# Filter taps joined in the array's rows, Hyena projections moved among the long convolutions, and attention maxima taken negated

## The chip, the core and the metric

One core of a Trainium2 chip (8 cores). The metric is the device time of one execution of the whole program in microseconds, the median of several runs. TensorE is PE in the profile, VectorE DVE, ScalarE ACT, GpSimd POOL, and SP is the queue that loads weights.

## The reference

Two transformer blocks run one after the other on 512 tokens of width 1024, all in float32. The parts that matter here lie in the second block.

Differential attention (4 heads, two maps each) over 256 context and 512 own keys:

```python
s = einsum("bhmqd,bhmkd->bhmqk", q, k) * (64 ** -0.5)     # 0.125
a = softmax(s)
w = a[:, :, 0] - lam * a[:, :, 1]
o = einsum("bhqk,bhkd->bhqd", w, v)                        # then rmsnorm, a gain
```

The Hyena mixer: a projection to 1536 columns (12 groups of 128, named 0 to 11 below), a short convolution of 3 taps, then a split into v, x1, x2 (groups 0 to 3, 4 to 7, 8 to 11) and two orders of a gated long convolution:

```python
for n, gate in enumerate((x1, x2)):
    z = gate * (long_conv(z, k_f[:, n]) + p["hy_skip"][n] * z)
```

Its filters come from a small network: 33 features of 512 positions, three layers of width 64 with a sine, and a last matrix 64 x 2048 (2 orders, 2 directions, 512 channels), times a decay. The filters do not depend on x, so they can be made at any time.

## The kernel before, in words

**Arithmetic and weights.** Big matrix products are made of fp32r matmuls. Each operand is a high part and a low part, and `mm3` issues three matmuls (high·high, high·low, low·high). Weights come in units of 128 x 1024 in one fixed order (`plan`, line 27), through four RAW buffers and four slots of WH and WL. SP loads RAW, ScalarE copies it to WH (line 1081, `wh`), and VectorE (line 1651) or GpSimd (line 2274) writes `wl` = RAW − WH. Which of the two does it is the list POOL_LOW (line 155). ScalarE, VectorE and GpSimd walk the units in order and stay SLOTS − 1 = 3 units ahead of TensorE. The DFT matrices of the long convolutions come already split (kind "pre", list PRE) and are loaded straight to WH and WL by GpSimd's queue (`load_pre`, line 2280), which waits until TensorE has begun the unit three before. Each engine has its program written out in its own order; semaphores join them.

**PSUM banks.** `bank(key, s, n, among)` (line 434) takes the next bank of a ring in fixed rotation and waits until semaphore `s` says that the bank's last user is drained. In the long convolutions there are two rings, RING4 = banks 0 to 3 and ACC = banks 4 to 7; Hyena groups 0 to 9 use RING2 = (6, 7).

**Filters (first block, 25 to 115 us).** While TensorE makes the projections of the first block, one step `first(k)` (24 fp32r matmuls) is followed by one step `second(k)`: three `filter_layer` (line 557, fp32, 64 output rows, 64 columns of weights), then eight `taps(i, o)` (line 567). Each of these has two fp32 matmuls of K = 64, 128 output rows and 512 columns, both from partitions 0 to 63. An fp32 matmul stands as two passes in the trace. VectorE multiplies by the decay (line 1718), GpSimd adds and subtracts the two directions (line 2311), SP stores them.

**Differential attention (945 to 1052 us).** 16 cycles n, one for each head and block of 128 queries. TensorE: `diff_scores(n)` (line 882; 64-row pairs, m = 0 and 1, into banks 0+1 and 2+3, free again after the exponentials), `diff_turn(n − 2)` (six transposes), two quarters of a Hyena group (12 matmuls, `hyena_part`, line 913), and once in four cycles `diff_values`. VectorE: `diff_max(n)` (line 2057: maximum of 768 scores, times −0.125, for each of the two maps), at times the split of a weight unit or `hyena_conv` (line 2078, the short convolution of a group in place in TMP), then `diff_weights(n)` (line 2066: `em` = em0 + r·em1, two SBUF inputs). ScalarE: `exp(0.125·s + bias)` (line 1444). GpSimd is idle. Eight groups (0 to 7) are done here.

**Long convolutions (1052 to 1166 us).** `hyena_turn(j)` transposes the convolved group j, ScalarE copies it to U. `fold(o)` makes even and odd parts `ED` of z, high and low (VectorE, ScalarE, GpSimd). Then for each order o and quarter f: `forward(o, f)` (12 matmuls, two RING4 banks, drained by the first four products), `spectral` on VectorE (line 2147: four products, a difference, a sum), high part `ysh` on ScalarE, low part `ysl` on GpSimd, and `backward(o, f)` (12 matmuls into the four ACC banks) two quarters later. At the end of an order z = gate · (...) on VectorE and GpSimd, then fold again. In between stand the attention output's scaling (`sub_sums`: 32 matmuls of one column; `sub_scale(h)`: one fp32 matmul with the diagonal `ndg` from ScalarE) and the Hyena groups 8 to 11 (`hyena_group`, line 937). TensorE's order before is:

```
turns 0-3, group 8, turns 4-7, sub_sums, group 9, turn 8
order 0: fw0 sc0 fw1 fw2 bw0 fw3 turn9 sc1 bw1 group10 bw2 bw3 group11 sc2
order 1: fw0 turn10 sc3 fw1 fw2 bw0 fw3 turn11 bw1 bw2 bw3
output projection: first half (48 matmuls), transposes of xn, second half
```

Of the kernel before, what the change touches and what calls it, by code (L numbers as in the profile page):

```python
# [9 lines left out]
P = 128  # L10
S = 512
D = 1024
# [6 lines left out]
BEFORE = 10  # L19
# [8 lines left out]
def plan():  # L28
# [69 lines left out]
    for o in range(2):  # L98
# [4 lines left out]
        if o == 0:  # L103
            pack(colmajor("w_in_2", 1536 + 10 * P, 1))
        pack(inv[2] + inv[3], "pre")
        if o == 0:
            pack(colmajor("w_in_2", 1536 + 11 * P, 1))
# [39 lines left out]
for _u in range(NU):  # L147
# [9 lines left out]
    AT["dft_f", 0, 0][0][0] + SLOTS - 1 <= u < AT["w_out_2", 0, 0][0][0] + SLOTS - 1  # L157
# [8 lines left out]
class Waits:  # L166
# [5 lines left out]
    def wait_ge(self, name, n):  # L172
        s, before = self.find(name)
        if n > 0 and self.past.get(s.name, 0) < before + n:
# [35 lines left out]
          "v_score": (("sb_sp", 32), ("df_mx", 64)),  # L210
# [61 lines left out]
def program(nc, a):  # L272
    ctx = ExitStack()
    with ctx:
# [54 lines left out]
        W4 = at("w4", 168, [64, CHUNK])  # L329
# [95 lines left out]
        def tensor_program(engine):  # L425
# [131 lines left out]
            def filter_layer(l):  # L557
# [405 lines left out]
            for j in range(4):  # L963
                hyena_turn(j)
            hyena_group(8)
            for j in range(4, 8):
                hyena_turn(j)
            sub_sums()
            hyena_group(9)
            hyena_turn(8)  # L970
# [24 lines left out]
            for o in range(2):  # L995
                for f in range(4):
                    forward(o, f)
                    if f == 0:
                        if o:
                            hyena_turn(10)  # L1000
                        sub_scale(3 * o)
                    if f == 3:
                        hyena_turn(9 + 2 * o)
                        if o == 0:
                            sub_scale(1)
                    if f >= 2:
                        backward(o, f - 2)
                if o == 0:
# [58 lines left out]
        def scalar_program(engine):  # L1067
# [65 lines left out]
            def second(k):  # L1133
                if k < 3:
                    e.wait_ge("f_red", 7 * k + 7)
                    act(TMP[0:64, (4, 5, 4)[k], :], TMP[0:64, 3, :], ACT.Sin).then_inc(sem("f_sin"), 1)
# [246 lines left out]
            def rotated(r):  # L1383
                e.wait_ge("rp_add", 2 * r + 2)
                dh = QTh[:, r, :] if r < 4 else KTh[:, r - 4, 256:]
                act(dh, T(2 + r % 3), ACT.Copy).then_inc(sem("qk2_hi"), 1)
# [51 lines left out]
            def diff_scores(n):  # L1438
                for m in range(2):
                    b = BANK["ds", 2 * n + m]  # L1440
                    s = PS[:, b:b + 2, :].rearrange("p a n -> p (a n)")[:, 0:768]
                    e.wait_ge("df_mx", 4 * n + 2 * m + 2)
                    e.wait_ge("p_dt", n - 1)
                    act(EM[n % 2][m][:, :], s, ACT.Exp, scale=0.125, bias=ND[n % 4][:, m:m + 1],  # L1444
# [52 lines left out]
            weights(unit("w_in_2", 0, 1536 + 8 * P) + SLOTS - 1)  # L1497
            conv_center(8)
# [4 lines left out]
            weights(unit("w_in_2", 0, 1536 + 9 * P) + SLOTS - 1)  # L1503
            conv_center(9)
            hyena_turn(8)
# [9 lines left out]
            for o in range(2):  # L1515
                for f in range(4):
                    weights(unit("dft_f", 128, f * P, o) + SLOTS - 1)
                    spectral(4 * o + f)
                    if f == 0:
                        if o:  # L1520
                            hyena_turn(10)
# [3 lines left out]
                    if f == 3:  # L1525
                        hyena_turn(9 + 2 * o)
                        if o == 0:
                            sub_high(1)
                            sub_diag(2)
                    if f >= 2:  # L1530
                        weights(unit("dft_i", 0, 0, o) + SLOTS - 1 if f == 2 else unit("dft_i", P, 0, o) + SLOTS - 1)
                if o == 0:
                    weights(unit("w_in_2", 0, 1536 + 10 * P) + SLOTS - 1)
                weights(unit("dft_i", 3 * P, 0, o) + SLOTS - 1)
                for i in range(2):
# [1211 lines left out]
```

## Time and profile before

| | |
|---|---|
| median of 3 runs | 1582.85 us (1582.1 to 1583.59) |
| profiled execution | 1580.21 us |
| its span, first to last instruction | 1578.5 us |
| mean granted TensorE clock | 0.991 of full speed |
| TensorE matmuls | 1507.5 us busy (96%), 6878 |
| VectorE | 877.3 us (56%), 1429 |
| ScalarE | 622.5 us (39%), 978 |
| GpSimd | 291.1 us (18%), 289 |
| memory | 187.87 MB moved, mean 119 GB/s |

Busy time is the time in which at least one instruction of the engine was running. TensorE's matmuls overlap, so the length of one is more than the distance between two; what one costs is the distance between starts. A number in square brackets behind a row is the idle time ahead of it and what ended it. `TMP<-PS,pp,TMP x6` is one short convolution, `TMP<-PS,kf x4` the four products of a spectral step.

### The profile page before, as it was taken

The numbers are of one execution on the slowest core, as the hardware profiler recorded it, in microseconds if no ns is written. First come the engines' busy times: TensorE is split into PE (matmuls) and PEld (weight loads), VectorE is DVE, ScalarE is ACT, GpSimd is POOL, SyncE is SP. The second block draws the span as 40 slices with busy tenths as digits, with TensorE's granted clock in tenths as the row PEclk, the third lists the DMA queues.
The fourth block names the chain that finished last, engine by engine and source line by source line (L and its number), as shares of the span: only waits on it lengthen the run. The fifth ranks groups of instructions, "written<-read, shape, count | busy, mean of one in ns | idle before, by whom it ended". The sixth has DMA issues, their size and how long they took to land.

```text
span 1578.5 us, 17718 instructions
## 1 busy us (share of the span) xinstructions
PE 1507.5 (96%) x6878; PEld 1200.0 (76%) x6878; DVE 877.3 (56%) x1429; ACT 622.5 (39%) x978; POOL 291.1 (18%) x289
## 2 busy tenths in 40 slices
PE   6999999999989999999997998989798999999998
PEld 5767667888868878888886876668576888888886
DVE  5445556555467654565447438856766455334534
ACT  5535664222353322334335325644344333223332
POOL 0253111110122200122004310006441110111101
PEclk9999999999999999999999999999999999999999
DMA  7342002654345544545326221124442322323221
GB/s 232 126 146 81 27 28 93 235 166 148 132 134 173 174 147 140 178 145 178 113 100 208 91 67 40 41 94 139 131 154 69 108 93 95 99 89 106 94 94 54
DMA packets 53262, 187.87 MB, mean 119 GB/s; under 512 B 6104, under 2 KB 6616, under 8 KB 52986
## 3 DMA queue, kind: packets, MB, share of 16 engines
q1 hardware_dynamic: 47386, 165.76, 32.3%
q0 software_dynamic: 4736, 16.78, 3.2%
q10 hardware_dynamic: 1056, 4.19, 0.7%
q8 instruction: 55, 0.90, 0.2%
q14 instruction: 29, 0.24, 0.0%
HBM read 174.12 MB, written 12.58 MB: 118 GB/s over the span
## 4 chain that ended last, share of the span: by engine, by line
PE 80%; DVE 9%; issue 4%; ACT 4%; POOL 3%; DMA 0%; SPq 0%; DVEq 0%; POOLq 0%; ACTq 0%
PE PS L447 79%; POOL TMP L2311 2%; DVE smallring L2062 1%; DVE TMP L2083 1%; PE PS L458 1%; ACT em L1444 1%; DVE wl L1651 1%; DVE TMP L2158 1%; DVE em L2076 1%; POOL y L2321 0%; DMA X<-in_x 0%; ACT wh L1081 0%; DVE accm L1631 0%; ACT wt L1435 0%; POOL wl L2274 0%
## 5 line engine op out<-in xcount | busy, mean ns | idle before, releaser
L1651 DVE TENSOR_TENSOR wl<-raw,wh 128x1024 fp32r<-128x1024 f32 x219 | 283.8, 1299 | 283.1 <-ACT wh L1081 283.0
L447 PE MATMUL PS<-HTh,wh 128*128 128x512 f32 x1056 | 419.7, 397 | 12.4 <-DVE TMP L1977 5.8
L447 PE MATMUL PS<-HTh,wl 128*128 128x512 f32 x1056 | 413.0, 391 | 0.0
L447 PE MATMUL PS<-HTl,wh 128*128 128x512 f32 x1056 | 412.8, 391 | 0.0
L1081 ACT ACTIVATE wh<-raw 128x1024 fp32r<-128x1024 f32 x228 | 239.1, 1053 | 286.2 <-PE PS L447 251.9
L447 PEld LDWEIGHTS PS<-HTh,wh 128*128 128x128 f32 x1056 | 199.5, 189 | 61.3 <-issue 11.0
L447 PEld LDWEIGHTS PS<-HTh,wl 128*128 128x128 f32 x1056 | 199.0, 188 | 42.8
L447 PEld LDWEIGHTS PS<-HTl,wh 128*128 128x128 f32 x1056 | 199.5, 189 | 38.5 <-issue 0.5
L447 PE MATMUL PS<-wh,FFh 128*128 128x512 f32 x432 | 169.1, 392 | 0.0
L447 PE MATMUL PS<-wh,FFl 128*128 128x512 f32 x432 | 168.2, 389 | 0.0
L447 PE MATMUL PS<-wl,FFh 128*128 128x512 f32 x432 | 168.1, 389 | 0.0
L1631 DVE SCALAR_TENSOR_TENSOR accm<-raw,small,accm 128x256 f32<-128x256 f32 x224 | 108.0, 516 | 3.4
L2234 DVE SCALAR_TENSOR_TENSOR TMP<-PS,pp,TMP 128x255 f32<-128x255 f32 (+1 forms) x132 | 52.1, 395 | 80.3 <-ACT TMP L1583 76.4
L447 PEld LDWEIGHTS PS<-wh,FFl 128*128 128x128 f32 x432 | 81.1, 188 | 17.1
L447 PEld LDWEIGHTS PS<-wl,FFh 128*128 128x128 f32 x432 | 81.1, 188 | 16.5
L447 PEld LDWEIGHTS PS<-wh,FFh 128*128 128x128 f32 x432 | 81.1, 188 | 16.5
L2384 POOL TENSOR_TENSOR FFl<-TMP,FFh 128x512 fp32r<-128x512 f32 x32 | 41.6, 1299 | 240.1 <-ACT FFh L1295 240.1
L2466 POOL TENSOR_TENSOR FFl<-TMP,FFh 128x512 fp32r<-128x512 f32 x22 | 28.5, 1294 | 211.8 <-ACT FFh L1590 211.8
L1295 ACT ACTIVATE FFh<-TMP 128x512 fp32r<-128x512 f32 x32 | 20.2, 632 | 66.5 <-DVE TMP L1917 66.5
L1291 ACT ACTIVATE TMP<-PS 128x512 f32<-128x512 f32 x32 | 19.0, 595 | 57.7 <-PE PS L447 57.7
L2083 DVE SCALAR_TENSOR_TENSOR TMP<-PS,pp,TMP 128x255 f32<-128x255 f32 (+1 forms) x72 | 28.4, 395 | 16.0 <-ACT TMP L1452 13.9
L2474 POOL TENSOR_TENSOR X<-X,TMP 128x512 f32<-128x512 f32 x14 | 19.7, 1434 | 90.1 <-DVE TMP L2249 90.1
(320 smaller groups left out, 2163.7 us busy)
## 6 DMA issues: line engine op xcount, KB each, us to landing
raw<-in_ws SPq DMA_DIRECT2D x268, 512.0 KB, 3.8
taps<-TMP SPq DMA_DIRECT2D x16, 256.0 KB, 2.5
tab<-in_spec POOLq DMA_DIRECT2D x8, 512.0 KB, 5.6
raw<-taps SPq DMA_DIRECT2D x8, 512.0 KB, 3.7
kd<-TMP POOLq DMA_DIRECT2D x16, 256.0 KB, 4.3
wh<-in_wd POOLq DMA_DIRECT2D x8, 512.0 KB, 3.9
wl<-in_wd POOLq DMA_DIRECT2D x8, 512.0 KB, 4.6
kf<-kd SPq DMA_DIRECT2D x8, 512.0 KB, 3.9
```

The lines of the kernel that those rows point to most:

```text
L447: return nc.tensor.matmul(out, l, r, start=start, stop=stop, skip_group_check=True)
L1081: act(WH[u % SLOTS][:, :n], RAW[i % RAWS][:, :n], ACT.Copy).then_inc(sem("w_hi"), 1)
L1291: act(T(q % 2), PS[:, BANK["ff", hf, m], :], ACT.Relu).then_inc(sem("ff_relu"), 1)
L1295: act(FFh[:, m, :], T(2 + q % 2), ACT.Copy).then_inc(sem("ff_hi"), 1)
L1631: stt(acc, r[:, k % 4, :], c, acc, ALU.mult, ALU.add).then_inc(sem("mod_acc"), 1)
L1651: tt(WL[k][:, :n], RAW[RAW_AT["unit", u, 0] % RAWS][:, :n], f32(WH[k][:, :n]), ALU.subtract).then_inc(sem("lo_dve"), 1)
L2083: stt(out[:, do], ps[:, di], pp("hy_conv_w_2", 12 * w + j), out[:, do], ALU.mult, ALU.add).then_inc(sem("hc_v"), 1)
L2234: stt(z[:, do], ps[:, di], pp("ffn_conv_w_2", 22 * w + m), z[:, do], ALU.mult, ALU.add).then_inc(sem("uc_v"), 1)
L2311: tt(T(k), T(3), T(5), op).then_inc(sem("tap_ed"), 1)
L2384: tt(FFl[:, q % 16, :], T(2 + q % 2), f32(FFh[:, q % 16, :]), ALU.subtract).then_inc(sem("ff_lo"), 1)
L2466: tt(FFl[:, m - first_m, :], T(m % 4), f32(FFh[:, m - first_m, :]), ALU.subtract).then_inc(sem("ug_lo"), 1)
L2474: tt(x, x, T(4 + q % 4), ALU.add).then_inc(sem("dn_xp"), 1)
```

## The change

1. **Taps.** The three layers' weights are laid twice side by side, so that each layer gives 128 output rows, the lower 64 a copy of the upper. The last matrix is laid out as 128 x 1024: direction 0 in partitions 0 to 63, direction 1 in 64 to 127. `taps(i, o)` takes both banks first and then issues one matmul from each half of the partitions.
2. **Maxima.** `reduce_max(..., negate=True)` writes the negated maximum, and the multiply by −0.125 is gone (32 instructions). The queries carry the 0.125 (a scale in an existing copy and in an existing subtraction).
3. **Hyena groups 8 to 11.** Group 8 goes to order 0 ahead of bw2; 9 and 10 behind bw3; 11 to order 1 ahead of bw2. The turns, the short convolutions and the units of weights follow. TensorE's new order:

```
turns 0-7, sub_sums
order 0: fw0 sc0 fw1 fw2 bw0 fw3 sc1 bw1 group8 bw2 bw3 turn8 group9 group10 sc2
order 1: fw0 sc3 fw1 turn9 fw2 turn10 bw0 fw3 bw1 group11 bw2 bw3 turn11
```

   On VectorE convolution 8 stands behind spectral step 3, 9 behind fold(1) and sub_high(2), 10 behind spectral step 4 and sub_high(3), 11 behind spectral step 7.
4. **POOL_LOW** begins at the first Hyena unit + 3 instead of the first DFT unit + 3.

```diff
 POOL_LOW = [u for u in range(NU) if u not in PRE and (
-    AT["dft_f", 0, 0][0][0] + SLOTS - 1 <= u < AT["w_out_2", 0, 0][0][0] + SLOTS - 1
+    AT["w_in_2", 0, 1536][0][0] + SLOTS - 1 <= u < AT["w_out_2", 0, 0][0][0] + SLOTS - 1
...
-        W4 = at("w4", 168, [64, CHUNK])
+        W4 = at("w4", 168, [P, D])
...
-                mm(PS[0:64, b, :], TMP[0:n, 1, 64 * l:64 * l + 64], src, True, True).then_inc(sem("p_filt"), 1)
+                mm(PS[:, b, :], TMP[0:n, 1, P * l:P * (l + 1)], src, True, True).then_inc(sem("p_filt"), 1)

             def taps(i, o):
+                n = 4 * i + 2 * o
                 for d in range(2):
-                    n = 4 * i + 2 * o + d
-                    b = bank(("tap", n), "tap_mul", n + 1, RING2)
-                    c = o * 1024 + d * 512
-                    e.wait_ge("f_sin", 3)
-                    e.wait_ge("d_w4", 48)
-                    mm(PS[:, b, :], TMP[0:64, 4, i * P:(i + 1) * P], W4[:, c:c + 512], True, True).then_inc(sem("p_tap"), 1)
+                    bank(("tap", n + d), "tap_mul", n + d + 1, RING2)
+                e.wait_ge("f_sin", 3)
+                e.wait_ge("d_w4", 48)
+                for d in range(2):
+                    pr = slice(64 * d, 64 * d + 64)
+                    mm(PS[:, BANK["tap", n + d], :], TMP[pr, 4, i * P:(i + 1) * P], W4[pr, o * S:(o + 1) * S], True,
+                       True).then_inc(sem("p_tap"), 1)
...
             def hyena_group(j):
-                bank(("hy", j), "hc_v", 6 * j + 6, RING2 if j < 10 else RING4)
+                bank(("hy", j), "hc_v", 6 * j + 6, ACC if j == 10 else RING4)
...
                     if f == 0:
-                        if o:
-                            hyena_turn(10)
                         sub_scale(3 * o)
-                    if f == 3:
-                        hyena_turn(9 + 2 * o)
-                        if o == 0:
-                            sub_scale(1)
+                    if f == 3 and o == 0:
+                        sub_scale(1)
+                    if f in (1, 2) and o:
+                        hyena_turn(8 + f)
                     if f >= 2:
                         backward(o, f - 2)
-                if o == 0:
-                    hyena_group(10)
+
+                hyena_group(8 + 3 * o)
                 backward(o, 2)
                 backward(o, 3)
+                hyena_turn(8 + 3 * o)
                 if o == 0:
-                    hyena_group(11)
+                    hyena_group(9)
+                    hyena_group(10)
                     sub_scale(2)
...
-                    nc.vector.reduce_max(r[:, m:m + 1], s, axis=mybir.AxisListType.X).then_inc(sem("df_mx"), 1)
-                    e.wait_ge("df_mx", 4 * n + 2 * m + 1)
-                    ts(r[:, m:m + 1], r[:, m:m + 1], -0.125, None, ALU.mult).then_inc(sem("df_mx"), 1)
+                    nc.vector.reduce_max(r[:, m:m + 1], s, axis=mybir.AxisListType.X, negate=True).then_inc(sem("df_mx"), 1)
...
                     spectral(4 * o + f)
                     if f == 0:
                         sub_high(3 * o)
+                    if f == 0 and o:
+                        hyena_conv(10)
                     if f == 3 and o == 0:
                         sub_high(1)
+                hyena_conv(8 + 3 * o)
                 e.wait_ge("p_bw", 4 * o + 4)
```

## Rows read from the trace of the kernel before

**Rows 1.** The page, part 1: busy us (share of the span) and instructions.

```profile
PE 1507.5 (96%) x6878; PEld 1200.0 (76%) x6878; DVE 877.3 (56%) x1429; ACT 622.5 (39%) x978; POOL 291.1 (18%) x289
```

**Rows 2.** Waits of TensorE: us in total, times, longest us.

```profile
PE PS L447 <- ACT em L1444: 7.8, 9, 1.0
...
PE PS L447 <- DVE TMP L2083: 6.0, 2, 5.0
...
PE PS L447 <- POOL ysl L2432: 3.0, 1, 3.0
```

**Rows 3.** Chain that ended last: start us, us, what.

```profile
760.38 8.20 PE PS L447 x36
```

**Rows 4.** Windows: PE, PEld, DVE, ACT, POOL busy, PEclk, DMA share, GB/s.

```profile
80.00:120.00 40.00, 40.00 (x151) 27.28 (x150) 18.11 (x22) 13.62 (x15) 22.24 (x17) 1.00 0.45 145
```

**Rows 5.** Timeline of PE around a pair of taps: start us, us, instruction.

```profile
65.16 1.98 PE L447 MATMUL PS<-w,TMP 64*128 64x512 f32 x4
67.07 0.50 PE L447 MATMUL PS<-HTh,wh 128*128 128x512 f32 x1
```

**Rows 6.** Timeline of PE around the pool's mixing.

```profile
131.77 1.07 PE L447 MATMUL PS<-pt,wpool 64*64 64x512 f32 x4
132.77 0.50 PE L447 MATMUL PS<-wh,HTh 128*128 128x512 f32 x1
```

**Rows 7.** Timeline of PE in attention, scores of two cycles.

```profile
998.10 0.50 PE L447 MATMUL PS<-KTh,QTh 64*128 64x512 f32 x2
...
1003.97 0.50 PE L447 MATMUL PS<-KTh,QTh 64*128 64x512 f32 x2 [1.01 <-ACT em L1444]
```

**Rows 8.** Timelines of DVE and ACT in the same cycle.

```profile
999.67 1.02 DVE L2076 SCALAR_TENSOR_TENSOR em<-em,smallring,em 128x768 f32<-128x768 f32 x1
1000.60 0.95 DVE L2062 TENSOR_REDUCE smallring<-PS 128x1 f32<-128x768 f32 x1
...
1001.66 0.95 DVE L2062 TENSOR_REDUCE smallring<-PS 128x1 f32<-128x768 f32 x1
...
997.84 1.06 ACT L1081 ACTIVATE wh<-raw 128x1024 fp32r<-128x1024 f32 x1
...
1002.83 0.90 ACT L1444 ACTIVATE em<-PS,smallring 128x768 f32<-128x768 f32 x1
```

**Rows 9.** Line 2274, GpSimd's splits: duration ns min/median/max.

```profile
L2274 POOL TENSOR_TENSOR wl<-raw,wh x9: 2358/2387/2844, 445.7 to 1151.7; 128x1024 fp32r<-128x1024 f32 x9
```

**Rows 10.** Line 1631, and timelines of DVE and POOL at 515 us.

```profile
L1631 DVE SCALAR_TENSOR_TENSOR accm<-raw,small,accm x224: 470/478/1526, 266.7 to 770.0; 128x256 f32<-128x256 f32 x112
...
515.01 2.55 DVE L1631 SCALAR_TENSOR_TENSOR accm<-raw,small,accm 128x256 f32<-128x256 f32 x3
...
515.45 1.30 POOL L2384 TENSOR_TENSOR FFl<-TMP,FFh 128x512 fp32r<-128x512 f32 x1 [3.88 <-ACT FFh L1295]
```

**Rows 11.** Timeline of PE, turns 0 to 3 and the transposes of xn.

```profile
1057.21 1.91 PE L458 MATMUL PS<-cst,TMP 128*128 128x128 f32 x16
...
1164.31 1.91 PE L458 MATMUL PS<-cst,xn 128*128 128x128 f32 x16
```

**Rows 12.** Timeline of PE in between, two waits and a slow matmul.

```profile
1071.12 0.63 PE L447 MATMUL PS<-HTl,wh 128*128 128x512 f32 x1
...
1126.95 2.07 PE L447 MATMUL PS<-ndg,cst 128*128 128x512 f32 x2 [5.01 <-DVE TMP L2083]
...
1150.58 0.50 PE L447 MATMUL PS<-ysh,wh 128*128 128x512 f32 x1 [3.05 <-POOL ysl L2432]
```

**Rows 13.** Timeline of DVE, a short convolution and four products.

```profile
1124.35 2.54 DVE L2083 SCALAR_TENSOR_TENSOR TMP<-PS,pp,TMP 128x255 f32<-128x255 f32 x6 [2.53 <-ACT TMP L1452]
1126.81 2.47 DVE L2158 TENSOR_TENSOR TMP<-PS,kf 128x512 f32<-128x512 f32 x4
```

**Rows 14.** Timelines of ACT and PE around the start of order 1.

```profile
1107.06 1.09 ACT L1537 ACTIVATE TMP<-PS 128x512 f32<-128x512 f32 x2 [5.14 <-PE PS L447]
...
1119.39 0.50 PE L447 MATMUL PS<-EDh,wh 128*128 128x512 f32 x1 [0.41 <-POOL EDl L2417]
```

More of the change, by code:

```diff
@@ L18 @@
 AHEAD = 8
-BEFORE = 10
+BEFORE = 8
 MAGIC = 12582912.0
@@ L961, in sub_scale @@
                 mm(PS[:, b, :], ONES, NDG[:, :], True, True).then_inc(sem("p_sn"), 1)
[L963 to L966, printed above, removed]
+            for j in range(8):
                 hyena_turn(j)
             sub_sums()
-            hyena_group(9)
-            hyena_turn(8)
             def forward(o, f):
@@ L1524, in scalar_program @@
                             sub_diag(1)
[L1525 to L1529, printed above, removed]
+                    if f == 3 and o == 0:
+                        sub_high(1)
+                        sub_diag(2)
+                    if f in (1, 2) and o:
+                        hyena_turn(8 + f)
                     if f >= 2:
                         weights(unit("dft_i", 0, 0, o) + SLOTS - 1 if f == 2 else unit("dft_i", P, 0, o) + SLOTS - 1)
-                if o == 0:
-                    weights(unit("w_in_2", 0, 1536 + 10 * P) + SLOTS - 1)
+                weights(unit("w_in_2", 0, 1536 + (8 + 3 * o) * P) + SLOTS - 1)
+                conv_center(8 + 3 * o)
                 weights(unit("dft_i", 3 * P, 0, o) + SLOTS - 1)
+                hyena_turn(8 + 3 * o)
                 for i in range(2):
@@ L1539, in scalar_program @@
                     fold(1)
-                    conv_center(10)
-                    weights(unit("w_in_2", 0, 1536 + 11 * P) + SLOTS - 1)
+                    weights(unit("w_in_2", 0, 1536 + 9 * P) + SLOTS - 1)
+                    conv_center(9)
+                    weights(unit("w_in_2", 0, 1536 + 10 * P) + SLOTS - 1)
                     sub_high(2)
                     sub_diag(3)
-                    conv_center(11)
+                    conv_center(10)
             e.wait_ge("p_bw", 8)
@@ L2014, in rotated @@
                 e.wait_ge("qk2_hi", r + 1)
-                tt(dl, T(2 + r % 3), f32(dh), ALU.subtract).then_inc(sem("qk2_lo"), 1)
+                if r < 4:
+                    stt(dl, T(2 + r % 3), 0.125, f32(dh), ALU.mult, ALU.subtract).then_inc(sem("qk2_lo"), 1)
+                else:
+                    tt(dl, T(2 + r % 3), f32(dh), ALU.subtract).then_inc(sem("qk2_lo"), 1)
             for m in range(4):
@@ L2125, in vector_program @@
             fold(0)
-            weights(unit("w_in_2", 0, 1536 + 8 * P) + SLOTS - 1)
-            hyena_conv(8)
             ps, fits, r, q = PS[:, BANK["sub"], 0:16], SUBR[:, 0:16], SUBR[:, 16:32], SUBR[:, 32:48]
@@ L2143, in vector_program @@
             stt(q, q, 1024.0, R0, ALU.mult, ALU.mult).then_inc(sem("sub_v"), 1)
-            weights(unit("w_in_2", 0, 1536 + 9 * P) + SLOTS - 1)
-            hyena_conv(9)
             def spectral(n):
@@ L2439, in gpsimd_program @@
                         weights(unit("dft_i", 0, 0, o) + SLOTS - 1 if f == 2 else unit("dft_i", P, 0, o) + SLOTS - 1)
-                if o == 0:
-                    weights(unit("w_in_2", 0, 1536 + 10 * P) + SLOTS - 1)
                 weights(unit("dft_i", 3 * P, 0, o) + SLOTS - 1)
                 e.wait_ge("ac_v", 4 * o + 2)
-                e.wait_ge("u_ev", 4 * o + 8)
+                e.wait_ge("u_ev", 8 if o == 0 else 12)
                 tt(U[:, 2, 0:512], T(4), U[:, 2, (o + 1) * S:(o + 2) * S], ALU.mult).then_inc(sem("z_p"), 1)
@@ L2447, in gpsimd_program @@
                     fold(1)
-                    weights(unit("w_in_2", 0, 1536 + 11 * P) + SLOTS - 1)
+                    weights(unit("w_in_2", 0, 1536 + 9 * P) + SLOTS - 1)
+                    weights(unit("w_in_2", 0, 1536 + 10 * P) + SLOTS - 1)
                     sub_low(2)
@@ L2584, in sync_program @@
             load_spectrum(1)
-            weights(unit("w_in_2", 0, 1536 + 9 * P) + SLOTS - 1)
             for n in range(8):
@@ L2593, in sync_program @@
                 if n == 3:
-                    weights(unit("w_in_2", 0, 1536 + 11 * P) + SLOTS - 1)
+                    weights(unit("w_in_2", 0, 1536 + 10 * P) + SLOTS - 1)
             weights(unit("w_out_2", 7 * P, S) + SLOTS - 1)
@@ L2731 @@
         "lam": np.concatenate([i[n].reshape(-1) for n in ("lam_q1_2", "lam_q2_2", "lam_k1_2", "lam_k2_2")]),
-        "hy_w1_2": i["hy_w1_2"][0], "hy_w2_2": i["hy_w2_2"][0], "hy_w3_2": i["hy_w3_2"][0],
-        "hy_w4_2": i["hy_w4_2"][0],
-    }
+        "hy_w4_2": i["hy_w4_2"][0].reshape(64, 2, 2, S).transpose(2, 0, 1, 3).reshape(P, D),
+    }
+    for n in ("hy_w1_2", "hy_w2_2", "hy_w3_2"):
+        arrays[n] = np.tile(i[n][0], (1, 2))
     arrays = {k: np.ascontiguousarray(v) for k, v in arrays.items()}
```

38 lines of the change are left out of this document (13 added, 25 removed).

## The prediction

> **What bounds the kernel now.** I started with the page: TensorE (PE) is busy 1507.5 of 1578.5 us, VectorE (DVE) 877 [rows 1]. So a microsecond taken off TensorE's own work, where it never waits, is a microsecond of the end, and the rest of what can be won is in its few waits. Then the waits by releaser, of which the change bears on three: 7.8 us for ScalarE's exponentials `em`, 6.0 us for VectorE's short convolutions (L2083), 3.0 us for GpSimd's `ysl` [rows 2]. A full fp32r matmul of 512 columns costs TensorE 0.228 us (36 in 8.20 us), however long its own bar is [rows 3]. Last, the timelines of three places: the filters' taps (65 to 111 us), differential attention (945 to 1052), the long convolutions (1057 to 1164).
>
> **Taps of the filters.** From 80 to 120 us TensorE is busy in all 40.00 us [rows 4], so its work there is the path. Two taps are four passes over the same 64 rows: the next matmul starts 67.07 − 65.16 = 1.91 us later [rows 5]. The nearest thing to the new form is the pool's mixing, also two fp32 matmuls of 512 columns from partitions 0 to 63 and 64 to 127, in the order pass, pass, pass, pass: 132.77 − 131.77 = 1.00 us for the four [rows 6]. It has other columns too, the taps have not; but the scores of attention are 64x128 pairs of exactly the taps' form, and there the two of a pair stand as "x2" at one start in 0.50 us together, five more such pairs behind them [rows 7]. Eight pairs × 0.91 = **7.3 us** off. Bounds: 0 (no overlap) and 8.0. The second bank is now waited for before the first matmul; it was drained while the whole projection before it ran (24 × 0.228 = 5.5 us), so nothing waits behind it. VectorE's filter steps on 128 partitions instead of 64, ScalarE's sines, and three wider loads cost the same per column and are hidden: 0. GpSimd's sums of taps follow the taps and move with them.
>
> **Maxima negated as taken.** Each of 32 small multiplies holds VectorE from one `reduce_max` to the next: 1001.66 − 1000.60 = 1.06 us, of a 0.95 us instruction whose follower could start 0.09 before its end, so 0.87 without. The second exponential starts at 1002.83 and TensorE's scores at 1003.97 after a wait of 1.01 [rows 8, 7]. Without both multiplies and with ScalarE's own 0.88 between exponentials, it starts some 0.36 us earlier from the same first maximum, and 0.27 more where two cycles hang on each other. Beside this the diff widens POOL_LOW: its lower end goes from the first DFT unit + 3 to the first Hyena unit + 3. So the five splits of Hyena units 3 to 7, in the midst of attention, go from VectorE to GpSimd, and those of units 8 and 9 leave attention with their units. Followed cycle by cycle, the waits on `em` shrink by 0.6 at four places, by 0.3 to 0.4 at two: **3.2 us** off, if GpSimd does not hurt. The 0.125 on the queries is folded into an existing copy and subtraction outside any wait: 0.
>
> **What GpSimd's splits take back.** One takes it 2.39 us [rows 9]. GpSimd is idle in attention, so by itself this is hidden. But a VectorE instruction with two SBUF inputs stops while GpSimd reads: three `accm` steps took 2.55 us from 515.01, with a GpSimd subtraction from 515.45 to 516.75; such a step is 0.478 us at the median and 1.526 at most [rows 10]. The weighting `em<-em,smallring,em` (L2076) is of that kind, 0.95 us, and on the path (it stands ahead of the next maxima). In the cycles with a convolution, ScalarE's `wh` begins at 997.84 and takes 1.06, GpSimd would start at 998.98 and read until 1001.4, and `em` starts at 999.67, after the change 0.27 earlier: 999.40, some 0.4 us behind GpSimd, and waits: 2.0 us late [rows 8, 9]. The pattern repeats: I find this order at three of the five `wh` rows of the stage (units 4, 5 and 7; the row shown is unit 7's) and the reverse at two (3 and 6), where GpSimd waits and nobody is late. 3 × 1.95 = 5.85 us. Attention is then 5.85 − 3.2 = **2.65 us slower**. The bounds are −3.2 (none) and +6.5 (all five, at 1.95).
> By the Trainium skill, "SBUF — State Buffer", section "Who interferes with whom", a VectorE instruction with two SBUF inputs contends with a GpSimd instruction that reads SBUF, and whichever issues first holds the port for the whole instruction; by that rule the price is the same 2 us each, and the trace's 1.526 us rows agree.
>
> **The long convolutions.** Turns 0 to 3 start at 1057.21, the transposes `xn` at 1164.31: 107.1 us [rows 11]. The work in between is 336 matmuls (four groups of 24, eight forwards and eight backwards of 12, 48 of the output projection) × 0.228 = 76.5, twelve turns 5.0, sub_sums 3.5, four sub_scales 3.7: 88.7. So 18.4 us are lost, mainly a wait of 5.01 before sub_scale(3), 3.05 before backward(1,2), and a stretch of 0.43 us a matmul instead of 0.23 at the lower clock (1.2 instead of 2.4 GHz) after sub_sums' small matmuls [rows 11, 12]. None of the 88.7 is removed; only the order is new.
> I laid the new order out against these durations: convolution of a group 2.54, products of a spectral step 2.47 (step about 4) [rows 13], ScalarE's copy of a turn 0.5.
> Start: with groups 8 and 9 gone, turns 4 to 7 wait for ScalarE's copies (1.3), the first forward for banks and the low halves (0.5), sub_scale(0) for `ndg`, which comes some 5.5 us after sub_sums ends (four turn copies and a table load now stand ahead of it on ScalarE, and group 9 no longer covers it). The low clock falls into the same gap. Loss 4.5.
> Order 0: group 8 covers spectral step 3, groups 9 and 10 with sub_scale(2) are 11.9 us of work after backward(0,3). What forward(1,0) needs came until 1119.39 after a copy begun at 1107.06 [rows 14]; 12.3 us; turn 8's copy, now ahead of it on ScalarE, makes it 13.4. That is the last low half, which the forward needs 2.1 us after its start, at 14.0. Covered, by 0.6: 0.
> Order 1: the four-bank ring decides. In the new order sub_scale(3) takes the bank after forward(1,0), so forward(1,1) straddles: its second half takes forward(1,0)'s first bank and waits 0.9 for the products; forward(1,2) takes sub_scale's (0.3) and then forward(1,1)'s first, free only after spectral step 5's products. VectorE now does convolution 9, step 4, sub_high(3), convolution 10, and only then step 5: 13.5 us. That wait is 3.6. Loss 4.8. The output projection's banks wait for turn 11's copy: 0.7. The end's chain (copy, products, norm) has 11 us of matmuls above it, as now.
> New losses 10.0 instead of 18.4: **8.3 us** off. Unknown ones: a ring wait of 0 to 7 us, a low clock of up to 2 us more; 5 to 12. GpSimd's loads of the DFT halves stand behind fold(1) and group 10's split; they land 4.6 us after issue, just in time.
>
> **The sum.** The profiled execution took 1580.2 us around a span of 1578.5; the median of three runs is 2.6 above it. −7.3 + 2.65 − 8.3 = −12.95: 1567.3 profiled, 1569.9 against 1582.85.
>
> **The rivals.** (a) *GpSimd never catches `em`.* It is 0.35 to 0.45 us early in my layout, so a small shift undoes it. Then 1569.9 − 5.85 = 1564.1. Chance 0.27. (b) *The taps do not overlap* (no pair of fp32 passes on 64x128 stands in the trace): 1577.2. Chance 0.05. (c) *VectorE sets the pace of order 1*, with both convolutions and its two-SBUF sums held up by GpSimd as in [rows 10]. Two or three blocks of 2 us more than I laid out are 4 to 5 us: 1574.5. Chance 0.09. (d) *Slower:* TensorE's clock falls after sub_sums and, with gaps where groups 8 and 9 stood, does not come back for some time. Each matmul then costs 0.2 more; 65 of them eat the gain, 81 make it 0.2% slower. Before, eight or nine like the one shown were slow there [rows 12]. All 288 to the end of order 1 would be 1627. Chance 0.02. The forecast itself: 0.57. That the change does less than it says is (b).
>
> **How the numbers follow.** The point is the forecast's, 1569.9. The range takes in (a) with its unknowns and the forecast's own spread by the order-1 wait, 1562 to 1574; outside are (b), (d), half of (c) and the tails. A measurement of this kernel can tell about 0.2% (3.2 us) from no change. Every case but (d) and a coincidence of (b) and (c) is faster by more: 0.96, 0.02 and 0.02.
>
> **What would show it.** Right: taps rows at 1.0 us before the next matmul; five GpSimd `wl` rows in attention, three of 16 L2076 rows near 3 us; PE waits on `em` of 2 us at two or three places; no wait before sub_scale(3) for L2083, but one of some 3.6 us for L2158 in forward(1,2); turns to `xn` in about 99 us. Wrong: all L2076 rows at 1.02 us; taps still 1.9; a row of slow matmuls past 1080.

## The result, and the profile after

The changed kernel takes 1574.3 us at the median (1570.36 to 1576.92, six runs) beside 1582.86 (1582.1 to 1583.59, six runs): ratio 0.9945, 95% interval 0.9933 to 0.9958, so 8.6 us faster. I had said 12.95 us, 1569.9 us, and a range of 1562 to 1574: the sign was right, the size was not, and the median lies just above the range. The profiled execution took 1573.92 us around a span of 1572.2. Between the two profiled executions the span falls by 6.3 us only, from 1578.5 us.

The page's first part, busy time and instructions, answers to [rows 1]:

```profile
PE 1508.3 (96%) x6878; PEld 1201.7 (76%) x6878; DVE 868.3 (55%) x1390; ACT 623.6 (40%) x978; POOL 307.6 (20%) x296
```

TensorE's busy time has not fallen, though the taps alone should have taken 7 us off it. That is the first sign that matmuls elsewhere became longer. GpSimd has 16.5 us more: seven more splits at about 2.4 us, five of them in attention and two in the long convolutions, where the units of groups 8 and 9 now fall. The waits of TensorE (total, times, longest) answer to [rows 2]:

```profile
PE PS L446 <- ACT em L1442: 9.7, 8, 2.2
...
PE PS L446 <- ACT TMP L1359: 3.9, 1, 3.9
PE PS L446 <- DVE TMP L2147: 3.9, 3, 3.2
```

The waits of 5.0 us for the short convolutions and of 3.0 us for `ysl` are gone, as meant. In their place stand 3.9 us for the products of a spectral step, and the wait for `em` has grown from 7.8 to 9.7 with a longest one of 2.2 instead of 1.0.

**Taps.** TensorE's timeline around the second and the last pair, which answers to [rows 5]:

```profile
63.28 1.13 PE L446 MATMUL PS<-w,TMP 64*128 64x512 f32 x4
64.34 0.50 PE L446 MATMUL PS<-HTh,wh 128*128 128x512 f32 x1
...
103.72 1.13 PE L446 MATMUL PS<-w,TMP 64*128 64x512 f32 x4
104.78 0.50 PE L446 MATMUL PS<-HTh,wh 128*128 128x512 f32 x1
```

The next matmul starts 1.06 us after the pair instead of 1.91. Eight pairs give 6.8 us.

**Attention.** TensorE, then VectorE and GpSimd around the third cycle:

```profile
958.91 0.50 PE L446 MATMUL PS<-KTh,QTh 64*128 64x512 f32 x2 [2.15 <-ACT em L1442]
...
972.04 7.08 PE L446 MATMUL PS<-wt,V 128*128 128x512 f32 x12
...
953.07 2.92 DVE L2069 SCALAR_TENSOR_TENSOR em<-em,smallring,em 128x768 f32<-128x768 f32 x1
955.91 1.81 DVE L2057 TENSOR_REDUCE smallring<-PS 128x1 f32<-128x768 f32 x2
...
952.79 2.39 POOL L2263 TENSOR_TENSOR wl<-raw,wh 128x1024 fp32r<-128x1024 f32 x1 [6.46 <-ACT wh L1079]
```

GpSimd's split starts 0.28 us ahead of the weighting, which then takes 2.92 us (1.02 in [rows 8]) and ends about as late as if it had begun behind the split. The next maxima stand behind it, then the exponentials, and TensorE waits 2.15 us. There are three such cycles (waits of 2.15, 2.13 and 2.15). The new thing is in the second row: the twelve matmuls of a value product take 7.08 us. They took 5.42 before. The windows of the changed kernel say why (busy time of PE, PEld, DVE, ACT and POOL; then the granted clock, the DMA share and GB/s):

```profile
965.00:975.00 10.00, 7.87 (x36) 5.27 (x35) 7.82 (x8) 2.69 (x5) 2.07 (x1) 0.85 0.14 52
995.00:1005.00 10.00, 7.84 (x42) 5.31 (x40) 8.24 (x11) 2.77 (x6) 2.39 (x1) 0.89 0.18 54
1050.00:1060.00 10.00, 8.83 (x28) 4.60 (x28) 1.38 (x3) 1.98 (x5) 0.00 (x0) 0.83 0.00 0
```

In part of each stretch TensorE runs at 1.2 instead of 2.4 GHz. Two of the three follow right behind a wait of over 2 us, and their value products take 7.08 and 7.11 us. The last one is the last value product, 7.09 us, with only the usual waits of under 1 us ahead. And the first of the three long waits, the one shown above, is followed by no such stretch. The same view right behind it, with two of TensorE's rows:

```profile
961.00:963.00 2.00, 2.00 (x11) 1.64 (x10) 1.96 (x4) 1.93 (x4) 0.00 (x0) 1.00 0.00 0
...
961.33 0.39 PE L446 MATMUL PS<-HTh,wl 128*128 128x512 f32 x1
961.56 0.39 PE L446 MATMUL PS<-HTh,wh 128*128 128x512 f32 x1
```

The matmuls there follow each other every 0.23 us, at the full clock. So a wait of this length does not always bring the clock down.

**The long convolutions.** TensorE's timeline: turns 0 to 3, the end of the first sub_scale, the start of order 1, its three waits with matmuls behind the last of them, the output projection and `xn`. It answers to [rows 11, 12]:

```profile
1057.19 1.91 PE L457 MATMUL PS<-cst,TMP 128*128 128x128 f32 x16
...
1072.68 0.79 PE L446 MATMUL PS<-EDh,wh 128*128 128x512 f32 x1
...
1110.37 1.02 PE L446 MATMUL PS<-ndg,cst 128*128 128x512 f32 x2
...
1117.02 0.51 PE L446 MATMUL PS<-EDh,wh 128*128 128x512 f32 x1 [0.42 <-DVE TMP L2147]
...
1120.05 0.50 PE L446 MATMUL PS<-EDh,wh 128*128 128x512 f32 x1 [0.93 <-DVE no L2116]
...
1124.90 0.50 PE L446 MATMUL PS<-EDh,wh 128*128 128x512 f32 x1 [3.19 <-DVE TMP L2147]
...
1126.21 0.63 PE L446 MATMUL PS<-EDl,wh 128*128 128x512 f32 x1
1126.63 0.63 PE L446 MATMUL PS<-EDh,wl 128*128 128x512 f32 x1
1127.06 1.05 PE L457 MATMUL PS<-cst,TMP 128*128 128x128 f32 x4
...
1148.83 0.47 PE L446 MATMUL PS<-wh,O2h 128*128 128x512 f32 x1 [0.73 <-issue]
...
1159.83 0.38 PE L457 MATMUL PS<-cst,xn 128*128 128x128 f32 x2
```

From 1057.19 to 1159.83 are 102.6 us instead of 107.1: 4.5 off, where I had 8.3. From 0.6 us behind the end of the wait of 3.19 us the matmuls follow each other every 0.42 us (1126.63 − 1126.21) instead of 0.228, until 1129.

The two traces side by side, stage by stage, as what the changed kernel adds or saves: up to the matmul behind the last tap −7.7 (the taps' stretch −6.7, the time ahead of it −1.1); from there to attention +0.6, where stretches at the lower clock fall differently; attention to the last value product +5.4; that product +1.7; long convolutions −4.5; the rest −1.8. The sum is −6.3.

### The profile page after: what moved, and what is told of

It is laid out like the page before. It is cut to its first block, busy times and chain, and to the rows that moved or that the text cites. A ratio compares the mean times of both kernels' runs of the same rounds, so it can differ in the third digit from the quotient of the medians.

```text
span 1572.2 us, 17694 instructions
## 1 busy us (share of the span) xinstructions
PE 1508.3 (96%) x6878; PEld 1201.7 (76%) x6878; DVE 868.3 (55%) x1390; ACT 623.6 (40%) x978; POOL 307.6 (20%) x296
## 4 chain that ended last, share of the span: by engine, by line
PE 81%; DVE 8%; ACT 4%; issue 4%; POOL 3%; DMA 0%; SPq 0%; DVEq 0%; POOLq 0%; ACTq 0%
PE PS L446 80%; POOL TMP L2300 2%; ACT em L1442 1%; DVE TMP L2076 1%; DVE em L2069 1%; PE PS L457 1%; DVE TMP L2147 1%; DVE smallring L2057 1%; DVE wl L1644 1%; POOL y L2310 0%; DVE TMP L1697 0%; DMA X<-in_x 0%; ACT wh L1079 0%; DVE accm L1624 0%; ACT wt L1433 0%
## 5 line engine op out<-in xcount | busy, mean ns | idle before, releaser
L1644 DVE TENSOR_TENSOR wl<-raw,wh 128x1024 fp32r<-128x1024 f32 x212 | 274.4, 1298 | 282.3 <-ACT wh L1079 281.9
L2223 DVE SCALAR_TENSOR_TENSOR TMP<-PS,pp,TMP 128x255 f32<-128x255 f32 (+1 forms) x132 | 52.1, 395 | 78.2 <-ACT TMP L1576 74.3
L2263 POOL TENSOR_TENSOR wl<-raw,wh 128x1024 fp32r<-128x1024 f32 x16 | 39.5, 2469 | 122.7 <-ACT wh L1079 122.7
```

The source lines that it names most:

```text
L1644: tt(WL[k][:, :n], RAW[RAW_AT["unit", u, 0] % RAWS][:, :n], f32(WH[k][:, :n]), ALU.subtract).then_inc(sem("lo_dve"), 1)
L2223: stt(z[:, do], ps[:, di], pp("ffn_conv_w_2", 22 * w + m), z[:, do], ALU.mult, ALU.add).then_inc(sem("uc_v"), 1)
L2263: tt(WL[k][:, :n], RAW[RAW_AT["unit", u, 0] % RAWS][:, :n], f32(WH[k][:, :n]), ALU.subtract).then_inc(sem("lo_pool"), 1)
```

## The experiments

Each kernel was timed beside the kernel before on the same chip; I give ratios to it, which can be compared across the groups. The first four kernels ran together (before: 1581.67 us).

**The filters' taps alone.** The kernel before with the change's hunks on the filter layers, `taps`, W4 and the host's tiling, nothing else (one of its hunks):

```diff
-                    mm(PS[:, b, :], TMP[0:64, 4, i * P:(i + 1) * P], W4[:, c:c + 512], True, True)
+                    mm(PS[:, BANK["tap", n + d], :], TMP[pr, 4, i * P:(i + 1) * P], W4[pr, o * S:(o + 1) * S], True, True)
```

> The kernel before with the taps alone joined. Theory: 8 pairs at 1.07 instead of 1.91 us, 6.7 us off with nothing taken back: 1576.2 us (1575 to 1577). Rival (what the taps give is lost again later, in a stage that waits for loads): 1578 to 1583 us, with TensorE's waits after 115 us longer than before.

Measured: 1574.25 us, ratio 0.9956 (0.9941 to 0.9971), 7.0 us faster, and just under the 1575 to 1577 us expected. Its last pair takes 1.13 us with the same rows as in the changed kernel. The term stands, a little under 7.3, since a pair is 1.06 and not 1.00.

**The order of the Hyena projections alone.** The hunks on groups, turns, convolutions and their weights' places:

```diff
-BEFORE = 10
+BEFORE = 8
...
-            for j in range(4):
-                hyena_turn(j)
-            hyena_group(8)
-            for j in range(4, 8):
+            for j in range(8):
                 hyena_turn(j)
             sub_sums()
-            hyena_group(9)
-            hyena_turn(8)
```

> The kernel before with the new order of Hyena groups 8 to 11 alone (units 8 and 9 leave attention with them). Theory by my layout: from turn 0 to the transposes of xn 98.8 us instead of 107.1, and 1574.6 us. As the changed kernel's own trace has it: 102.6 us in that stage with 3 to 4 us of it at the low clock, and 1577 to 1580 us. The wait before the second half of forward(1,2) is 3 to 4 us in both. Rival (most of the 8.3 us is lost to the ring): the stage at 105 us or more, 1581 to 1584 us.

Measured: 1576.14 us, ratio 0.9962 (0.9948 to 0.9977), 6.0 us faster, and just under the 1577 to 1580 us expected. It has the waits of 0.44, 0.91 and 3.19 us in order 1, the last one without any split moved and without the maxima: the ring's wait belongs to the order. From turn 0 to `xn` it takes 102.6 us, as the changed kernel does. It also has the −1.8 us behind the long convolutions, which the expectation left out.

**The splits alone.** The kernel before, with the splits of Hyena units 3 to 7 on GpSimd:

```diff
     AT["dft_f", 0, 0][0][0] + SLOTS - 1 <= u < AT["w_out_2", 0, 0][0][0] + SLOTS - 1
+    or AT["w_in_2", 0, 1536][0][0] + SLOTS - 1 <= u < AT["w_in_2", 0, 1536 + 8 * P][0][0]
```

> The kernel before with the splits of Hyena units 3 to 7 alone given to GpSimd. Theory (lock): two or three of the 16 weightings are near 3 us long, TensorE's waits on em grow from 7.8 us to 11 or more, and the kernel is 3 to 8 us slower: 1586 to 1591 us. Rival (VectorE is relieved of five splits and nothing else happens): 1580 to 1583 us.

Measured: 1589.9 us, ratio 1.0053 (1.0038 to 1.0068), 8.4 us slower. The waits for `em` of this version, the weighting of its exponentials (L2077; duration in ns: shortest, median, longest), and windows of TensorE alone (busy time, granted clock, DMA share, GB/s):

```profile
PE PS L448 <- ACT em L1445: 10.7, 8, 2.5
...
L2077 DVE SCALAR_TENSOR_TENSOR em<-em,smallring,em x16: 1017/1019/3178, 953.1 to 1058.4; 128x768 f32<-128x768 f32 x16
...
960.00:980.00 20.00, 17.47 (x98) 0.91 0.09 33
980.00:1000.00 20.00, 16.67 (x81) 1.00 0.08 23
1000.00:1020.00 20.00, 17.48 (x86) 0.91 0.16 52
```

TensorE's three longest waits for `em` end at 969.75 (2.50 us), 982.65 (1.58) and 1011.82 (2.52). The three long weightings take 2.54, 3.18 and 2.52 us. The clock falls in the two windows with a wait of 2.5 us, not in the one with 1.58. In the kernel before, with waits of up to 1.01 us, it is 1.00 from 945 to 1057.

**The splits back.** The changed kernel with the old lower bound of `POOL_LOW`, all else as changed:

```diff
-    AT["w_in_2", 0, 1536][0][0] + SLOTS - 1 <= u < AT["w_out_2", 0, 0][0][0] + SLOTS - 1
+    AT["dft_f", 0, 0][0][0] + SLOTS - 1 <= u < AT["w_out_2", 0, 0][0][0] + SLOTS - 1
```

> The changed kernel with POOL_LOW's old lower bound: the splits of Hyena units 3 to 7 in attention are VectorE's again; all else stays changed. Theory (VectorE's two-input weighting em stops while GpSimd reads SBUF): the three waits of TensorE of 2.13 to 2.15 us on em shrink to under 0.6, all 16 weightings are 1.02 us long, and from the first scores to the last values (112.3 us in the changed kernel) it takes 104.5 to 107. If TensorE's low clock in attention is a sequel of these waits, its matmuls of the first two value products are back at 5.4 us each and the kernel is at 1563 to 1568 us. Rival (the low clock comes by chance, wherever): it stays as often as it was and the kernel is at 1568 to 1571 us. Rival (GpSimd's splits cost nothing, the stage is slow for another reason): 1573 to 1576 us.

Measured: 1563.63 us, ratio 0.9881 (0.9864 to 0.9897). One line of the change, taken back, gives some 10 us: the ratios differ by 0.0064, which is 10.1 us. From the view of waits and from the timeline and the groups of its VectorE, with the value product and the weighting of this version:

```profile
PE PS L446 <- ACT em L1442: 3.6, 7, 0.9
...
970.66 5.42 PE L446 MATMUL PS<-wt,V 128*128 128x512 f32 x12
...
L2069 DVE SCALAR_TENSOR_TENSOR em<-em,smallring,em 128x768 f32<-128x768 f32 x16 | 16.3, 1019 | 0.6
```

The weighting takes 16.3 us in all; in the changed kernel the same group takes 22.0. So the stops are 5.7 us, my 5.85. But from the first score to the last value product this version needs 104.2 us and the changed kernel 112.3, and that product is 1.7 longer besides: 9.8 us. What is beyond 5.7 is the clock. Two value products inside the stage are 1.66 and 1.69 us longer, and the last one 1.70: 5.0. Together these are 10.7, and 0.9 goes the other way. The traces show where: behind the wait of 1.97 us ahead of the first scores, this version ran at the lower clock and the changed kernel did not. TensorE's rows of this version, then those of the changed kernel:

```profile
939.33 0.79 PE L446 MATMUL PS<-KTh,QTh 64*128 64x512 f32 x2 [1.97 <-DVE V L2031]
...
945.07 0.50 PE L446 MATMUL PS<-KTh,QTh 64*128 64x512 f32 x2
```

```profile
937.93 0.50 PE L446 MATMUL PS<-KTh,QTh 64*128 64x512 f32 x2 [1.98 <-DVE V L2031]
...
942.65 0.50 PE L446 MATMUL PS<-KTh,QTh 64*128 64x512 f32 x2 [0.42 <-ACT em L1442]
```

From the first scores to the second are 5.74 us here and 4.72 there, 1.0 us.

**Is it the moment, or the engine?** Those two runs show that the five splits cost 8 to 10 us on GpSimd, not that their moment is to blame. So the next version leaves them on GpSimd and only has each start behind the weighting of its cycle:

```diff
+                        first = AT["w_in_2", 0, 1536][0][0] + SLOTS - 1
+                        if first <= u < AT["dft_f", 0, 0][0][0]:
+                            e.wait_ge("df_w", 2 * (u - first) + 1)
                         e.wait_ge("w_hi", highs(u))
```

> The changed kernel with one wait more: each of the five splits that GpSimd took over in the attention first waits until VectorE has weighted the exponentials of its cycle (counts 1, 3, 5, 7, 9). No work is moved between engines. Theory A (the loss is the meeting of the GpSimd split and the weighting, which stops VectorE for some 2 us in three cycles, and TensorE's clock falls after the wait that this makes): the weighting is 1.02 us in all cycles, no wait for it over 1 us, the value products 5.4 us each, the time about that of the version with the splits back on VectorE or a little under it, 1561 to 1565 us, -9 us or more against the changed kernel. Rival B (GpSimd slows the other VectorE instructions as well, the maxima or the filter's taps, wherever the split lies, or the split comes too late for its matmuls): 1568 to 1574 us, and the stopped instructions have other lines or TensorE waits for the low halves.

Measured (before in this group: 1581.72 us): 1564.8 us, ratio 0.9895 (0.9882 to 0.9908), 7.9 us under the changed kernel by the ratios. GpSimd's second split, with its releaser, and the weighting of this version:

```profile
957.80 2.40 POOL L2266 TENSOR_TENSOR wl<-raw,wh 128x1024 fp32r<-128x1024 f32 x1 [7.61 <-DVE em L2069]
...
L2069 DVE SCALAR_TENSOR_TENSOR em<-em,smallring,em x16: 1017/1019/1021, 946.7 to 1041.8; 128x768 f32<-128x768 f32 x16
```

The same five splits take the same 2.40 us each, no weighting is longer than 1.021 us, no wait for `em` is over 0.9 and no value product takes more than 5.42 us. Theory A holds: the loss was in which of the two started first. Leaving the splits on GpSimd brings nothing over the splits on VectorE either, 1564.8 and 1563.6, so GpSimd was not needed here.

**The maxima alone.** In the kernel before, with the 0.125 moved to the queries as in the change:

```diff
-                    nc.vector.reduce_max(r[:, m:m + 1], s, axis=mybir.AxisListType.X)
-                    ts(r[:, m:m + 1], r[:, m:m + 1], -0.125, None, ALU.mult)
+                    nc.vector.reduce_max(r[:, m:m + 1], s, axis=mybir.AxisListType.X, negate=True)
```

> The kernel before with the maxima alone: the scores scaled by 0.125 where the rotated queries are cut, the maximum negated as it is taken, one VectorE instruction less per maximum (32 in all). My sum priced this part and the fewer splits on VectorE at -3.2 us together. Theory A (the exponentials wait for the maximum, so each saved row of about 0.15 us lies on the path of a cycle, two a cycle): the six waits of TensorE for the weighted exponentials fall from about 1.0 to 0.25 us in three cycles and by 0.3 in others, in all -2 to -3.5 us against before, ratio about 0.998. Rival B (the cycle is set by TensorE's own work, the saved rows only lengthen VectorE's idle time): -0.5 to 0 us, ratio 1.000. Between first score and the last value product the trace would show 104 us under A and 107 us under B.

Measured: 1578.25 us, ratio 0.9982 (0.9971 to 0.9992), 2.8 us faster by the ratio. The waits for `em` fall from 7.8 to 3.5 us in all:

```profile
PE PS L447 <- ACT em L1444: 3.5, 7, 0.9
```

From the first score to the last value product it takes 104.3 us instead of 107.0, although its first cycle ran in part at the lower clock (5.74 us from the first scores to the second, 5.08 before). Theory A holds.

**The ring of banks.** The splits back, and in order 1 sub_scale(3) and turn 9 take a bank of the accumulators instead of the forward transforms' four; turn 10 moves behind the second backward, and ScalarE copies turn 9 ahead of the spectral step:

```diff
-                b = bank(("ht", j), "u_ev", j + 1, RING4)
+                b = bank(("ht", j), "u_ev", j + 1, ACC if j == 9 else RING4)
...
-                b = bank(("sn", h), "sn_v", h + 1, RING4 if h % 2 else ACC)
+                b = bank(("sn", h), "sn_v", h + 1, RING4 if h == 1 else ACC)
...
-                    if f in (1, 2) and o:
-                        hyena_turn(8 + f)
+                    if f == 1 and o:
+                        hyena_turn(9)
                     if f >= 2:
                         backward(o, f - 2)
+                    if f == 3 and o:
+                        hyena_turn(10)
```

> The changed kernel with the splits of the attention back on VectorE, and in the second convolution's order the norm's sum and projection turn 9 moved from the ring of four PSUM banks to the accumulators' four, turn 10 on TensorE moved behind the second inverse transform, turn 9 on ScalarE ahead of the second spectral step. Theory A (my prediction's 3.6 us ring wait was the price of the order chosen: the third forward transform waits for a bank that the second spectral step holds, 0.42, 0.93 and 3.19 us, after which VectorE in its turn waits 1.5 and 2.9 us for TensorE): the three waits fall to under 1 us together, from the first forward transform to the last turn 4 to 6 us go, 1557 to 1560 us beside 1563.6 with the ring as it was. Rival B (VectorE and the split of the spectral steps bound this order: the inverse transforms wait for their low halves instead): at least half of the wait comes back in front of the inverse transforms, -0 to -2 us, 1561.5 to 1564.

Measured: 1561.16 us, ratio 0.9868 (0.9856 to 0.9881), 1 us above theory A's range and 2.1 us under the version with the splits back by the ratios. TensorE's timeline, the one wait that is left, ahead of the first backward of order 1, and the end of the stage:

```profile
1112.97 0.50 PE L446 MATMUL PS<-ysh,wh 128*128 128x512 f32 x1 [1.34 <-DVE TMP L2078]
...
1144.93 0.81 PE L457 MATMUL PS<-cst,xn 128*128 128x128 f32 x6
```

From the last value product to `xn` it takes 102.5 us instead of 107.9, 5.4 less, in the middle of theory A's 4 to 6. The span falls by 3.8 only, since 2.1 us were given back at one place, the wait of the feed-forward network for its first bank. The row of the version with the splits back, and then of this one:

```profile
1195.61 0.79 PE L446 MATMUL PS<-HTh,wh 128*128 128x512 f32 x1 [3.87 <-ACT TMP L1359]
```

```profile
1191.22 0.80 PE L446 MATMUL PS<-HTh,wh 128*128 128x512 f32 x1 [5.99 <-ACT TMP L1361]
```

VectorE's and ScalarE's rows between the transposes and this matmul are the same in both, at the same distances. Only the bank differs. The first feed-forward group takes bank 5 by its own rotation, and how often the long convolutions used their two sets of four banks decides which chunk's transposes lie in it: the seventh of eight before, the sixth after the change, the eighth here. The chunks are emptied in that order. So the 1.8 us that the change wins behind the long convolutions are this too: its wait is 3.88 instead of 5.83 us.

**Both.** GpSimd's splits behind the weighting, and the ring of banks as above.

> Both of the above: GpSimd splits behind the weighting, and the ring of banks as changed. If each theory A holds and the parts are in different stretches they add: 1555 to 1559 us. If the splits on GpSimd cost something in the stretch behind the attention, it is over the ring version's time. Under both rivals B 1566 to 1572 us.

Measured: 1561.56 us, ratio 0.9868 (0.9854 to 0.9883), the same as with the splits on VectorE, and 2 us above what I expected, for the wait just shown.

**The first bank of the feed-forward network.** One edit, in the kernel before and in the version with the ring (before in this group: 1582.17 us):

```diff
-                        b = bank(("up", m, q), "uc_v", 7 * m + (6 if q == 0 else 7))
+                        b = bank(("up", m, q), "uc_v", 7 * m + (6 if q == 0 else 7), order if m == 0 else None)
```

> The kernel before with one edit at a place that the change does not touch: the first two groups of the feed-forward network take the PSUM banks of the transposes that are emptied first, not banks 5 and 6 by the rotation. Theory C (the wait in front of these groups goes by which chunk stood in bank 5: the seventh of eight before, the sixth after the change, the eighth in the version with the ring of banks moved, with waits of 5.83, 3.88 and 5.99 us): with the first chunk in their bank TensorE starts with the chunk's low half, some 1 to 2 us after the transposes, waits in pieces for the next ones and ends the first group 2.5 to 4 us earlier, 1578 to 1579.3 us beside 1581.7. Rival D (the group is bounded by the last low half, whatever its bank, the wait only moves into the group): 0 to -0.5 us.

> The version with the ring of banks moved (1561.2 us) with the same edit. Theory C: its wait of 5.99 us is the longest of all, the edit gives 2.5 to 4.5 us, 1557 to 1559 us, and is the fastest of all versions. Rival D: 1560.5 to 1561.5.

Here `order` names the banks in the order in which they are emptied. Measured: in the kernel before 1579.65 us, ratio 0.9983 (0.997 to 0.9995), 2.7 us faster; with the ring 1557.37 us, ratio 0.9848 (0.9831 to 0.9865), 3 us under the ring alone by the ratios. The three waits that stand for the one of 5.83 us in the kernel before with this edit:

```profile
1207.93 0.47 PE L447 MATMUL PS<-HTh,wh 128*128 128x512 f32 x1 [1.25 <-DVE TMP L1977]
...
1209.69 0.79 PE L447 MATMUL PS<-HTh,wh 128*128 128x512 f32 x1 [0.83 <-POOL HTl L2462]
...
1214.56 0.50 PE L447 MATMUL PS<-HTh,wh 128*128 128x512 f32 x1 [0.44 <-POOL HTl L2462]
```

Theory C holds. This last version is the fastest: 1557.4 us beside 1582.2 of before and, by the ratios, 15 us under the changed kernel.

## Why the prediction was off

- **Taps: right.** −7.3 forecast; −6.7 in the trace, −7.0 alone.
- **Maxima: right.** −3.2 forecast with the splits that leave VectorE; −2.8 alone, and from the first score to the last value product it takes 104.2 us instead of 107.0 in the version with the splits back, where 1.0 of it is the lower clock at the start, and 103.2 with the late splits, which began at full clock.
- **GpSimd's splits: the mechanism right to the cycle, the price wrong.** Three of five splits (units 4, 5 and 7) meet the weighting, as laid out, and stop it for 5.7 us in all; I had 5.85. This was the likeliest case against rival (a), in which none meets. But I took the wait's length as its whole price. Behind two of the three waits TensorE fell to 1.2 GHz, and the value products there took 1.7 us more each; a third product, with no long wait ahead, did too. The forecast for attention was +2.65; measured are +5.4 and, with the last product, +7.1. The splits alone cost 8.4 us instead of 5.85. The step that failed is "3 × 1.95 = 5.85 us", and the bound of +6.5 under it was one for the stops, not for their consequences.
- **Long convolutions: the waits right in all, the sum 3.8 short.** By the prediction's own prices of matmuls, turns, sub_sums and sub_scales, the losses are 5.0 us in the start (1057.19 to 1072.68 less 10.5 of work; I had 4.5, and sub_sums itself took 4.83 us instead of 3.63), 0.8 in order 0 (to 1110.37, less 36.9; I had 0) and 8.1 in order 1 (to 1159.83, less 41.4; I had 4.8 and 0.7). In order 1 the waits shown are 0.42, 0.93, 3.19 and 0.73, 5.3 us, against 0.9, 0.3, 3.6 and 0.7 forecast, 5.5; the first two were off in opposite directions. Of the other 2.8 us, 1.7 are matmuls at the lower clock right behind the longest wait: from 1124.90 to 1131.16 are 6.26 us for 18 matmuls and a turn, 4.52 by the prediction's prices. The step that failed is again that a wait was booked at its own length. "A low clock of up to 2 us more" stood in the list of unknowns, with no value in the sum.
- **Not looked at:** the 1.8 us behind the long convolutions. I had written that the order was all that is new there, and had not followed the bank that the next stage would get.
- Rival (c) gave 1574.5 us, next to the measured 1574.3, but that is a coincidence: it asked for further waits in order 1, and there they come to 5.3 us against 5.5 forecast.
- Rivals (b) and (d) did not occur: the pairs overlap, and the matmuls are back at full clock by 1130.

Together the terms miss by +0.64 for the taps, +4.43 for attention with its last product and +3.84 for the long convolutions; −1.07 ahead of the taps and −1.82 from the bank go the other way, and +0.63 stands between the taps and attention. That is +6.65, from −12.95 to the −6.3 of the two profiled executions. The medians lie 8.6 us apart: the profiled execution of before was 2.7 us under its median, that of the changed kernel 0.4.

The Trainium skill, "SBUF — State Buffer", section "Who interferes with whom", was right here in both directions. By it, issue order decides which of the two engines blocks. The trace agrees: the weighting issued 0.28 us behind the split took 2.92 us. Where the weighting issued first, at 984.91, it took 1.02 us, and the split issued at 985.39 took 2.78 us instead of 2.39:

```profile
984.91 1.02 DVE L2069 SCALAR_TENSOR_TENSOR em<-em,smallring,em 128x768 f32<-128x768 f32 x1
...
985.39 2.78 POOL L2263 TENSOR_TENSOR wl<-raw,wh 128x1024 fp32r<-128x1024 f32 x1 [18.32 <-ACT wh L1079]
```

Open is what exactly brings the clock down. The last value product of the changed kernel ran at the lower clock with only waits of under 1 us right ahead of it, and the same waits left it at 5.39 us in all the other versions. The wait of 2.15 us that ends at 958.91 was followed by the full clock, those of 2.13 and 2.15 us ahead of two value products by the lower one. And one and the same wait, of 1.97 to 2.00 us ahead of the first scores of attention, stands in all twelve traces: matmuls at the lower clock follow it in five of them (splits back, splits alone, maxima alone, order alone, ring) and not in seven. Of the five waits for `em` of 2.13 to 2.52 us in the changed kernel and in the version with the splits alone, four were followed by the lower clock. So the longer waits were followed by it more often here, but the length of a wait alone does not decide it. No run was made that leaves such a wait in place and changes only its length. What is shown is that value products longer than 5.42 us stand only in the two versions in which GpSimd's splits meet the weighting, and that they are gone when the order of the two is turned.

## What to carry to other kernels

When work moves to an idle engine, ask which instruction of the others will be running when it starts, and order the two: the same five splits cost 8 to 10 us in front of the weighting and nothing behind it. Do not price a new wait in front of TensorE at its length alone: look for the granted clock behind waits of that length elsewhere in the trace, and cost the matmuls behind it at both levels (here 1.7 us for twelve, behind 2.15), as a chance and not as a certainty. And a rotation of banks couples stages that share nothing else: after any change of order, look at which bank the next stage's first group gets.

## What the runs showed of the hardware

- Two fp32 matmuls on 64 rows each, in different halves of the array's rows and issued one behind the other, take 1.06 us for four passes of 512 columns, instead of 1.91.
- A VectorE instruction of 1.02 us with two inputs in SBUF that issued behind a GpSimd subtraction took 2.92 to 2.93 us, and 2.52 to 3.18 in the version with the splits alone. A subtraction that issued 0.48 us behind such an instruction took 2.78 us instead of 2.39, and the instruction its 1.02.
- Behind two waits of 2.13 and 2.15 us, twelve matmuls of a value product ran in part at 1.2 GHz and took 7.08 and 7.11 us; behind waits of up to 1.01 us they took 5.42 in the kernel before. Behind 3.19 us the matmuls came every 0.42 us for some 4 us. Behind another wait of 2.15 us, and in seven of twelve traces behind one of about 1.97, they kept the full clock.
- The changed kernel's six runs spread over 6.6 us and those of before beside them over 1.5, but the kernel before spread over 6.2 and 9.4 us in two other groups of 17 runs.
